# Starting places of the matmul operands modulo 512 bytes in a four-layer float32 network on one core

## What is computed

```python
def swiglu(u, w_in, w_out):
    a, v = jnp.split(u @ w_in, 2, axis=-1)
    return (jax.nn.silu(a) * v) @ w_out

def ffn_sublayer(h, shift, scale, gate, w_in, w_out, g, b):
    y = swiglu(modulate(h, shift, scale), w_in, w_out)
    return layer_norm(ALPHA * h + FFN_RES * gate * y, g, b)
...
for i in range(DEPTH):      # first part, 2 layers: ffn, attention, ffn; hidden width 2,816
    h_lat = ffn_sublayer(h_lat, ...); h_ctx = ffn_sublayer(h_ctx, ...)
    y_lat, y_ctx = neighborhood_attention(...) if i % 2 == 0 else window_gqa(...)
    ...
```

## The kernel before

| tile | before | after |
|---|---|---|
| raw0, raw1 | 128 | 128 |
| whi0 / whi1 | 128 / 128 | 128 / 0 |
| wlo0 / wlo1 | 128 / 128 | 0 / 128 |
| h, squares, sums, scaled, full_u, k1 | 128 | 128 |
| uhi / ulo | 416 / 416 | 0 / 256 |
| fhi / flo | 416 / 416 | 64 / 448 |
| qT, kT, vv, q_parts, k_parts | 416 | 256 |
| u2hi / u2lo | 416 / 416 | 32 / 256 |
| yhi / ylo | 416 / 416 | 288 / 288 |
| f2hi / f2lo, mhi / mlo | 352 / 352 | 224 / 224 |

## Time and profile before

### The profile page before, as it was taken

How to read it: one execution, slowest core, us unless ns; L and a number is a source line. 1 busy time by engine, 2 the same in 40 slices (tenths; PEclk the granted TensorE clock), 3 DMA queues, 4 the chain that set the end, 5 groups by cost and what they waited for, 6 DMA issues and landing times.

```text
span 2618.0 us, 43371 instructions
## 1 busy us (share of the span) xinstructions
PE 2574.1 (98%) x17000; PEld 2287.9 (87%) x17000; DVE 1688.2 (64%) x2582; ACT 1093.9 (42%) x1560; POOL 445.0 (17%) x491
## 2 busy tenths in 40 slices
PE   8999999999999999999999999999999999999999
PEld 6888888867888888888889889989999999998999
DVE  6766747466674474675574876666866666675565
ACT  4222224265422222321223674345655555565453
POOL 4000024122500003400004232020201201100210
PEclk9999999999999999999999999999999999999999
DMA  7554523411253252354452225445433554542554
GB/s 297 169 184 154 190 106 132 159 65 49 97 197 132 97 202 79 129 197 149 146 191 76 88 76 190 177 153 222 164 128 125 182 192 173 194 160 81 180 188 156
DMA packets 64762, 394.40 MB, mean 151 GB/s; under 512 B 7552, under 2 KB 9056, under 8 KB 29664
## 3 DMA queue, kind: packets, MB, share of 16 engines
q1 hardware_dynamic: 43872, 317.17, 33.9%
q0 software_dynamic: 20192, 73.21, 8.5%
q10 hardware_dynamic: 544, 1.88, 0.2%
HBM read 391.19 MB, written 1.05 MB: 150 GB/s over the span
## 4 chain that ended last, share of the span: by engine, by line
PE 89%; DVE 5%; ACT 3%; issue 1%; DMA 1%; POOL 1%; SPq 0%; DVEq 0%; ACTq 0%; POOLq 0%
PE banks L459 24%; PE banks L461 23%; PE banks L460 23%; DVE wlo L384 2%; ACT whi L376 2%; PE banks L479 1%; PE banks L481 1%; PE banks L480 1%; PE banks L1787 1%; PE banks L1774 1%; DMA scale_start<-in_w_mod_scale 1%; PE banks L598 1%; PE banks L599 1%; PE banks L600 1%; PE banks L1763 1%
## 5 line engine op out<-in xcount | busy, mean ns | idle before, releaser
L384 DVE TENSOR_TENSOR wlo<-raw,whi 128x2048 fp32r<-128x2048 f32 (+1 forms) x262 | 641.0, 2447 | 341.1 <-ACT whi L376 341.0
L376 ACT CAST whi<-raw 128x2048 fp32r<-128x2048 f32 (+1 forms) x264 | 533.8, 2022 | 387.4 <-PE banks L461 355.3
L459 PE MATMUL banks<-uhi,whi 128*128 128x512 f32 (+2 forms) x1520 | 552.4, 363 | 2.9 <-DVE sums L2091 1.5
L460 PE MATMUL banks<-ulo,whi 128*128 128x512 f32 (+2 forms) x1520 | 551.3, 363 | 0.0
L461 PE MATMUL banks<-uhi,wlo 128*128 128x512 f32 (+2 forms) x1520 | 551.3, 363 | 0.0
L459 PE MATMUL banks<-u2hi,whi 128*128 128x256 f32 x1248 | 351.5, 282 | 2.1 <-DVE wlo L384 2.0
L460 PE MATMUL banks<-u2lo,whi 128*128 128x256 f32 x1248 | 348.5, 279 | 0.0
L461 PE MATMUL banks<-u2hi,wlo 128*128 128x256 f32 x1248 | 348.3, 279 | 0.0
L643 DVE SCALAR_TENSOR_TENSOR squares<-mod_slot,crow 128x1024 f32<-128x1024 f32 x256 | 313.3, 1224 | 31.0 <-DMA mod_slot<-in_w_mod 7.7
L459 PEld LDWEIGHTS banks<-uhi,whi 128*128 128x128 f32 x1520 | 285.6, 188 | 54.1 <-issue 1.8
L461 PEld LDWEIGHTS banks<-uhi,wlo 128*128 128x128 f32 x1520 | 285.6, 188 | 50.1
(11 more groups left out here) (482 smaller groups left out, 4885.3 us busy)
## 6 DMA issues: line engine op xcount, KB each, us to landing
raw<-in_ffn_in SPq DMA_DIRECT2D x132, 1024.0 KB, 4.8
raw<-in_ffn_out SPq DMA_DIRECT2D x48, 1408.0 KB, 6.2
mod_slot<-in_w_mod POOLq DMA_DIRECT2D x128, 512.0 KB, 3.7
raw<-in_w_merge SPq DMA_DIRECT2D x32, 1024.0 KB, 4.8
raw<-in_w_in SPq DMA_DIRECT2D x26, 1024.0 KB, 4.7
raw<-in_na_qkv SPq DMA_DIRECT2D x12, 1024.0 KB, 4.7
raw<-in_w_out SPq DMA_DIRECT2D x8, 1024.0 KB, 4.7
raw<-in_wa_qkv SPq DMA_DIRECT2D x6, 1024.0 KB, 4.8
```

Source lines behind the costliest of these rows:

```text
L376: act.copy(whi[u % 2][:, 0:unit_size[u]], raw[u % 2][:, 0:unit_size[u]]).then_inc(hi_done, 1)
L384: dve.tensor_tensor(wlo[u % 2][:, 0:n], raw[u % 2][:, 0:n], whi[u % 2][:, 0:n].bitcast(F32), ALU.subtract).then_inc(lo_done, 1)
L459: pe.matmul(out, w_hi, x_hi[:, k, 0:T], start=(n == 0), stop=False)
L460: pe.matmul(out, w_hi, x_lo[:, k, 0:T], start=False, stop=False)
```

## The change

Nine tiles get an `ahead` or lose it. Nothing else in the program changes: the same instructions in the same order with the same waits, at other addresses.

```diff
-    whi = [sb(f"whi{i}", [P, FC * 256], F32R) for i in range(2)]
-    wlo = [sb(f"wlo{i}", [P, FC * 256], F32R) for i in range(2)]
+    whi = [sb(f"whi{i}", [P, FC * 256], F32R, ahead=384 * i) for i in range(2)]
+    wlo = [sb(f"wlo{i}", [P, FC * 256], F32R, ahead=128 * i) for i in range(2)]
...
-    uhi = sb("uhi", [P, KC, T2], F32R, scope=block1)
-    ulo = sb("ulo", [P, KC, T2], F32R, scope=block1)
+    uhi = sb("uhi", [P, KC, T2], F32R, scope=block1, ahead=96)
+    ulo = sb("ulo", [P, KC, T2], F32R, scope=block1, ahead=256)
...
-    fhi = sb("fhi", [P, FC, T2], F32R, scope=ffn1_mem)
-    flo = sb("flo", [P, FC, T2], F32R, scope=ffn1_mem)
+    fhi = sb("fhi", [P, FC, T2], F32R, scope=ffn1_mem, ahead=320)
+    flo = sb("flo", [P, FC, T2], F32R, scope=ffn1_mem, ahead=384)
...
-    u2hi = sb("u2hi", [P, KC, S], F32R, scope=block2, ahead=384)
-    u2lo = sb("u2lo", [P, KC, S], F32R, scope=block2)
-    yhi = sb("yhi", [P, KC, S], F32R, scope=block2)
+    u2hi = sb("u2hi", [P, KC, S], F32R, scope=block2)
+    u2lo = sb("u2lo", [P, KC, S], F32R, scope=block2, ahead=224)
+    yhi = sb("yhi", [P, KC, S], F32R, scope=block2, ahead=32)
```

## The result

The changed kernel takes 2,625.93 us, the median of 12 runs (2,624.55 to 2,629.09), against 2,620.95 us for 12 runs of the kernel before on the same chip (2,617.07 to 2,622.87). The ratio is 1.0026, with a 95% interval of 1.0017 to 1.0034: slower by a quarter of a per cent. That is small, but the fastest run of the changed kernel is slower than the slowest of before. The medians themselves are 5.0 us apart. The profiled execution has a span of 2,627.2 us, 9.2 us above the 2,618.0 of before; at 2,628.93 us it was the second slowest of the 12.

What follows compares the result with a forecast made beforehand. The prediction took PE to be bound by the pace of its own matmuls. Its terms, 3.1 + 3.3 + 0.9 + 1.6 + 4.1 = 13.0 us, on the 2,618.0 us span plus 3.3 us gave 2,634.3 us; range 2,600 to 2,650.

Steps and rivals of the forecast that it cites:

- no effect of places: Rival: pace differences come from instruction forms, so new addresses change nothing; 2,621 us, chance 0.20.
- The choice of 128: All streams: assumed that the pace law, by moving start minus start of the weights loaded meanwhile, repeats modulo 128.
- point 5: 512-wide products on u and f, 4,452 matmuls: any weight-load slowdown hides in the longer step, 0 us.
- point 1: Products on uhi and ulo slow down: 256-wide 3.1 us, 258-wide 3.3 us, turned-round products (L598) 0.9 us.
- points 2 to 4: 256-wide products: f slower by 1.6 us; u2, a third of its matmuls slowed, 4.1 us; y, f2 and m 0.
- 12.8 us of loss as the bound: 512-wide products: if the moving stream is what slows, u pays 10.8 us and f 2.0 us.
- It has as much again to hide in: 512-wide step: whatever slows a weight load, which fits into a 116.4 ns 256-wide step, stays hidden; 0 us.
- it is wrong if this pace moves at all: Sign of error: any move of the 512-wide pace, which carries 1,040 us; each nanosecond is 4.5 us.
- the bound for gains: 512-wide products: running as freely as the half-rate ones (216 ns), 4,452 matmuls would gain 76 us.
- the new places are better: Rival: most new differences are faster for 256-wide products, 2,605 us, or 2,591 with the 512-wide; chance 0.30.
- the pace belongs to regular phases: Rival: mixed places keep 256-wide streams from settling, costing 9.2 us, 2,630.5; chance 0.50 shared with the difference law.

Runs made afterwards that it cites:

- e7_shift64: Kernel before with every tile, weights and moving alike, 64 bytes further on, all differences kept; 2,619.38 us in one run.
- e6_map_d: Kernel before with all weights at 128 and differences u 384, f 448, u2 352, y 480, f2 288, m 224; 2,621.94 us in one run.
- the maps: Five kernels, against the kernel before: all weights at 128, each moving stream at one other difference per kernel; 2,590.43 to 2,621.94 us, one run each.
- e2_moving_only: Changed kernel's moving tiles at their new places, all four weight buffers at 128 as in the kernel before; 2,623.84 us, ratio 1.0015.
- e9_lo_apart: Kernel before with whi at 128, wlo at 0, moving u at 128, f 192, u2 and y 64, f2 and m 320; 2,593.82 us in one run.
- e8_best_places: Kernel before with all weights at 128 and differences u 0, f 64, u2, y, f2 and m 192; 2,581.14 us, ratio 0.9863.

## Why the prediction was right or wrong

The sign was right, the time (2,634.3 forecast, 2,625.93 measured) is 8.4 us lower than forecast and inside the range. The forecast of +13.0 us met +5.0 between the medians, and +9.2 between the two profiles, of which some 3.3 are the clock. The prediction read the clock as at its upper level throughout; the 27.6 us at half of it are missing there, and so is the second largest wait (6.9 us, ahead of the 5.6 on wlo). Neither changes the reading that led to the forecast, and that reading held: PE bound by the pace of its own matmuls, DVE, ACT and the waits without a part, the pace set by the difference of places. e7_shift64 and the exchange in e6_map_d show the last. The rival "no effect of places" is out by the same two. The two plain float32 steps from which the prediction has it that a slower-fed stream loses nothing are 0.21 us apart to the hundredth only; by their start times such steps take 215 to 216 ns, 2 above the 213.3.

By the Trainium skill ("TensorE: Matmul & The Clock Gate", Part 2) a weight load has a read port of its own and steals no read bandwidth from the running matmul. Taken as a rule for the time, as the prediction weighed it, this would have made all these kernels equal, and there the runs disagree: 226.8 against 233.4 ns for one instruction, by addresses alone. Whether the ports have to do with it is not shown. The 215.8 ns that the prediction has from that page ("Back-to-back issue gap") are there the gap of an isolated matmul, so what lies above them is no measure of what places cost in a stream; the lowest pace seen here for 512 columns is 226.8.

The law taken for it was wrong in its period. The choice of 128 ("this is a choice, not a reading") is a step that failed; the period is 256. The other one is the 0 for the 512-wide products (point 5). That the 256-wide came to 12.7 us against 13.0 is luck: point 1 was 3.8 us too high and points 2 to 4 together 3.5 too low. Step by step:

1. *uhi and ulo, +7.3 us for the 256- and 258-wide and L598; measured +3.5.* The prediction put all the 256-wide at the pace of L553, 120.0, and the 258-wide 3.3 ns above their own. Half of the differences are 128 modulo 256, and there the maps have 118.9, not 120.0. The 258-wide have 120.4 to 120.8 at 0 and 121.2 to 122.2 at 128, and took 121.67. Of L598 only 0.1 us came of 0.9: the maps have 119.93 for it at 0 and 118.67 or 119.50 at 128, and its 118.53 after lies below all of them. Why is not explained.
2. *fhi and flo 256-wide, +1.6; measured +2.6.* No row showed this place. The differences are 64 and 192 modulo 256, the very places of the fastest paces (113.3), so the maps (114.6 to 116.1) say a gain of 1.1 to 2.6 ns, and the changed kernel has a loss of 1.95. By the weights at rest the difference goes 192, 64, 64 in even and 64, 192, 192 in odd units; by those loaded meanwhile, as the prediction counts, it stays at 192 in even and at 64 in odd units. The stream runs at 119.18, above either of the two paces that it has at fixed differences, and the steps of the matmuls on flo are the longest (120.4 ns against 118.4 to 118.8). With the moving tiles alone (e2_moving_only) it runs at 117.79. The e9_lo_apart streams u2 and f2 also go between 64 and 192 within a unit and keep 113.5 to 113.6; there only the weights' place changes, here the moving tile's too. So it takes both, and why stays open.
3. *u2, +4.1; measured +4.4.* The number is right and the reason is not. It was to be a third of the matmuls at 120.0 and the rest unchanged. By the measured table the six differences of two units (to the weights at rest; to those loaded meanwhile they are the same six in another order) are 160, 128, 32, 32, 0 and 160, with 118.1, 118.8, 116.9, 116.9, 119.8 and 118.1: a mean of 118.1, and 117.98 was measured.
4. *y, f2 and m, 0; measured +2.2.* The assumption that 32 equals 160 and 96 equals 224 was modulo 128. y by the table is (116.9 + 118.1) / 2 = 117.5, and 118.51 was measured, so 1.0 ns of it is not in the table; f2 is (120.0 + 118.3) / 2 = 119.15, and 119.50 was measured.
5. *512-wide, 0 with 12.8 us of loss as the bound; measured -3.5.* "It has as much again to hide in" is refuted by every map: this width moves most, 226.8 to 233.4. The prediction said that it is wrong if this pace moves at all, and that is where 3.5 us of error sit. The kernel before has both 512-wide streams at the slow end, so no placement could cost there, and the bound for gains was the one that mattered. By the table u512 would have been 229.6 (a gain of 12 us) and f512 231.2 (2.5 us); 232.33 and 233.15 were measured. The 2.7 ns between are the mixing inside a unit, nearly step by step what e9_lo_apart has (2.4 ns in the mean).

So had the table held for the 512-wide streams, with everything else as measured, the change would have gained about 2 us net instead of losing 9.2: the rival "the new places are better" was near for the 512-wide and wrong for all of the 256-wide. The rival "the pace belongs to regular phases" is partly right: mixing costs inside a unit. But its size was for the 256-wide alone, and much of what the 256-wide lost is the table's (u2, the largest, wholly). That its 9.2 us are the 9.2 of the span is chance.

## What to carry to other kernels

Where PE is busy 98% with `fp32r` matmuls, the start-to-start pace of each stream as a function of (moving start minus weights start) modulo 256 is worth measuring early; here nothing but `ahead` values lies between 2,626 and 2,581 us. Keep that difference the same for all the products of a unit, choose it for each width by itself (0 for 512 columns, 64 or 192 for 256 columns on these runs), and don't scatter the places. A quantity that one layout shows at a single value, as the 512-wide pace here, can't be held at nothing in a forecast: in e8_best_places it is 26.5 of the 40.4 us. And before two profiles are subtracted, the time each spent at the lower clock has to be added up; a line of nines doesn't show it.

## What the runs showed of the hardware that was not expected

- A 128x512 `fp32r` matmul behind another takes 226.8, 229.0, 232.4 or 233.3 ns at difference 0, 64, 128 or 192 modulo 256, and 233.3 to 233.4 at 32, 96 and 224. All are above the 213.3 ns of 512 columns at 2.4 GHz. 160 wasn't tried for this width.
- For 256 columns: 119.8 at 0, 116.7 to 117.2 at 32, 120.0 at 96, 118.6 to 118.9 at 128, 117.9 to 118.4 at 160, 118.3 at 224. At 64 and 192 there are two paces, 113.3 and 117.8 ns. What picks one was not found.
- Where the weights at rest and those loaded meanwhile lie at different places, both count (232.4 and 234.2 ns by line in e9_lo_apart, against 226.7 where both are at difference 0). Whether the matmul ahead has a part in it isn't told apart, and the physical cause is not shown. That it has to do with the two reads, of moving operand and weights, from one memory is a guess.
- The loss from mixing places is measured and its cause not known: 2.4 ns for u512 and 1.5 for f512 in e9_lo_apart, none for u512 and 0.8 for f512 from unit to unit, 1.0 for y and 1.4 to 4.6 for the f 256 stream of the changed kernel.
- Every kernel has a few short stretches at half the clock, 13.7 to 34.1 us in all, though its PEclk line is all nines; some 40 small products took 9.6 us in one of them and 6.6 us at the upper level.
